# Stick-breaking logs: block 0's three all-ones products become one product over a sum made beforehand

## The reference

```python
z = jnp.einsum('bhtd,bhsd->bhts', q_blk, k_pre) * scale
log_not = jnp.where(valid, jax.nn.log_sigmoid(-z), 0.0)
after = lax.cumsum(log_not, axis=3, reverse=True) - log_not
a = jnp.where(valid, jnp.exp(jax.nn.log_sigmoid(z) + after), 0.0)
outs.append(jnp.einsum('bhts,bhse->bhte', a, v_pre))
```

## Time and profile before

| | |
|---|---|
| median of 3 runs | 1830.77 us (1830.52 to 1831.32) |
| the profiled execution: time | 1831.15 us |
| its span in the profile | 1829.3 us |
| mean granted TensorE clock | 0.997 of full speed |
| instructions | 27260 |

### The profile page before, as it was taken

The page is one execution under the profiler, slowest core; times in us unless marked ns, Lnnn a source line. Parts: engine busy times, 40 slices in busy tenths (PEclk is TensorE's granted clock), DMA queues, the critical chain, the costliest instruction groups (busy, mean ns, idle before and its releaser), DMA issues.

```text
span 1829.3 us, 27260 instructions
## 1 busy us (share of the span) xinstructions
PE 1799.5 (98%) x10778; PEld 1594.2 (87%) x10778; DVE 1281.3 (70%) x1741; ACT 812.4 (44%) x1027; POOL 179.3 (10%) x97
## 2 busy tenths in 40 slices
PE   9999999999999999999999999999999999999996
PEld 8898989887888878788888999998898888999995
DVE  7566665753654737446587878887898786888786
ACT  5666666533223323224453343344545752343342
POOL 2000000010000000000001234230000001224310
PEclk9999999999999999999999999999999999999998
DMA  5012111132222221222512322322476412232331
GB/s 187 26 67 70 46 46 47 47 127 81 70 86 86 83 89 46 92 70 92 183 51 92 116 92 92 115 93 95 113 185 179 144 70 93 97 111 92 103 105 46
DMA packets 25986, 170.25 MB, mean 93 GB/s; under 512 B 2736, under 2 KB 5040, under 8 KB 6320
## 3 DMA queue, kind: packets, MB, share of 16 engines
q1 hardware_dynamic: 24176, 156.51, 24.5%
q0 software_dynamic: 1728, 12.58, 3.3%
HBM read 154.40 MB, written 2.10 MB: 86 GB/s over the span
## 4 chain that ended last, share of the span: by engine, by line
PE 90%; DVE 5%; ACT 2%; issue 2%; DMA 0%; POOL 0%; DVEq 0%; SPq 0%; ACTq 0%
PE psum L705 28%; PE psum L707 28%; PE psum L706 28%; DVE normed L1992 1%; PE psum L907 1%; PE psum L902 1%; PE psum L1049 1%; DVE h L2082 1%; ACT w_hi L1334 1%; PE psum L856 0%; ACT X_hi L1334 0%; PE psum L928 0%; PE psum L1255 0%; DMA h<-in_xfm 0%; ACT std L1334 0%
## 5 line engine op out<-in xcount | busy, mean ns | idle before, releaser
L705 PE MATMUL psum<-X_hi,w_hi 128*128 128x512 f32 (+2 forms) x1392 | 463.7, 333 | 2.8 <-issue 1.2
L707 PE MATMUL psum<-X_hi,w_lo 128*128 128x512 f32 (+2 forms) x1392 | 457.3, 329 | 0.0
L706 PE MATMUL psum<-X_lo,w_hi 128*128 128x512 f32 (+2 forms) x1392 | 457.2, 328 | 0.0
L1975 DVE TENSOR_TENSOR w_lo<-w_raw,w_hi 128x2048 fp32r<-128x2048 f32 x121 | 278.5, 2303 | 93.8 <-ACT w_hi L1334 93.4
L1334 ACT ACTIVATE w_hi<-w_raw 128x2048 fp32r<-128x2048 f32 x133 | 253.6, 1907 | 186.7 <-PE psum L707 149.6
L705 PEld LDWEIGHTS psum<-X_hi,w_hi 128*128 128x128 f32 x1392 | 262.6, 189 | 30.6 <-issue 5.9
L706 PEld LDWEIGHTS psum<-X_lo,w_hi 128*128 128x128 f32 x1392 | 263.0, 189 | 25.9 <-issue 2.4
L707 PEld LDWEIGHTS psum<-X_hi,w_lo 128*128 128x128 f32 x1392 | 262.5, 189 | 23.5
L705 PE MATMUL psum<-M_hi,w_hi 128*128 128x512 f32 x320 | 124.6, 389 | 0.0
L706 PE MATMUL psum<-M_lo,w_hi 128*128 128x512 f32 x320 | 124.6, 389 | 0.0
L707 PE MATMUL psum<-M_hi,w_lo 128*128 128x512 f32 x320 | 124.5, 389 | 0.0
(11 more groups left out here) (364 smaller groups left out, 3989.8 us busy)
## 6 DMA issues: line engine op xcount, KB each, us to landing
w_raw<-in_units SPq DMA_DIRECT2D x140, 1024.0 KB, 4.9
w_lo<-w_raw POOLq DMA_DIRECT2D x12, 1024.0 KB, 6.9
h<-in_xfm SPq DMA_DIRECT2D x4, 528.0 KB, 5.6
h<-in_xfm SPq DMA_DIRECT2D x1, 2112.0 KB, 9.3
decay<-in_dec SPq DMA_DIRECT2D x4, 512.0 KB, 5.6
out<-h SPq DMA_DIRECT2D x4, 264.0 KB, 2.3
out<-h SPq DMA_DIRECT2D x2, 496.0 KB, 2.9
rot<-in_consts SPq DMA_DIRECT2D x1, 528.0 KB, 6.9
```

The source lines that it names most:

```text
L705: nc.tensor.matmul(dst, w2[0], x2[0], start=first, stop=False, skip_group_check=True)
L706: nc.tensor.matmul(dst, w2[0], x2[1], start=False, stop=False, skip_group_check=True)
L707: m = nc.tensor.matmul(dst, w2[1], x2[0], start=False, stop=last, skip_group_check=True)
L1975: v.tensor_tensor(lo, w_raw[at.ring(j)][:, :], as_f32(hi), ALU.subtract).then_inc(w_lo_ready, 1)
```

## The change

Blocks 1 to 3 are now added up ahead of block 0's products: `later2` adds block 3 to the end of block 2, `later1` adds that to the end of block 1, in place in `sp`. The 384 columns that come out are split into `later_hi` (a new copy on ScalarE, into the 48 spare columns of each of the 8 rows of the `X_lo` buffer) and `later_lo` (a new subtraction on VectorE, at the place of `a_f`). Block 0 then has its triangle and one all-ones product with each of the two. The sum for the meta tokens needs one more addition, `all`, in place of three.

```diff
@@ logs, on TensorE
-            for b in (1, 2, 0):
-                pe.wait_ge(hd_dve.sem, hd_dve.at("sp_lo1" if b else "sp_lo0", g))
...
-                for b2 in range(b + 1, BLOCKS):
-                    c0 = P * (b2 - b)
-                    for x in (sp_hi, sp_lo):
-                        m = nc.tensor.matmul(psum[:, 4 + b, c0:c0 + KEY_LEN[b2]], cmat[:, C_ALL, :],
...
+            add_to(2, P, C_ALL, sp_hi, sp_lo, slice(KEY_OFF[3], PACKED)).then_inc(*hd_pe.step("logs1"))
+            pe.wait_ge(hd_dve.sem, hd_dve.at("sp_lo0", g))
+            add_to(0, 0, C_TRI, sp_hi, sp_lo, slice(0, KEY_OFF[1]))
+            pe.wait_ge(hd_dve.sem, hd_dve.at("later_lo", g))
+            nc.tensor.matmul(psum[:, 4, P:SEQ], cmat[:, C_ALL, :], later_hi, start=False, stop=False, skip_group_check=True)
+            nc.tensor.matmul(psum[:, 4, P:SEQ], cmat[:, C_ALL, :], later_lo, start=False, stop=False,
+                             skip_group_check=True).then_inc(*hd_pe.step("logs0"))
@@ softplus, on ScalarE, at its end
+            act.wait_ge(hd_dve.sem, hd_dve.at("later1", g))
+            a(later_hi, sp[:, SEQ:SEQ + LATER].rearrange("p (a b) -> p a b", a=DT), ACT.Copy).then_inc(*hd_act.step("later_hi"))
@@ weights, on ScalarE
-            act.wait_ge(hd_dve.sem, hd_dve.at("all3", g))
+            act.wait_ge(hd_dve.sem, hd_dve.at("all", g))
@@ softplus, on VectorE, behind between()
-            for n, cols in ((1, slice(SEQ, PACKED)), (0, slice(0, SEQ))):
+            def low(n, cols):
                 dve.wait_ge(hd_act.sem, hd_act.at(f"hi{n}", g))
                 v.tensor_tensor(sp_lo[:, cols], sp[:, cols], as_f32(sp_hi[:, cols]), ALU.subtract)\
                     .then_inc(*hd_dve.step(f"sp_lo{n}"))
+
+            def behind(b):
+                own = slice(KEY_OFF[b] + P, KEY_OFF[b + 1])
+                v.tensor_tensor(sp[:, own], sp[:, own], sp[:, KEY_OFF[b + 1]:KEY_OFF[b + 1] + KEY_LEN[b + 1]], ALU.add)\
+                    .then_inc(*hd_dve.step(f"later{b}" if b else "all"))
+            low(1, slice(SEQ, PACKED))
+            dve.wait_ge(hd_dve.sem, hd_dve.at("sp_lo1", g))
+            behind(2)
+            dve.wait_ge(hd_dve.sem, hd_dve.at("later2", g))
+            behind(1)
+            low(0, slice(0, SEQ))
+            dve.wait_ge(hd_act.sem, hd_act.at("later_hi", g))
+            tiles = [x.rearrange("p (a b) -> p a b", a=DT) for x in (later_lo, sp[:, SEQ:SEQ + LATER])]
+            v.tensor_tensor(tiles[0], tiles[1], as_f32(later_hi), ALU.subtract)\
+                .then_inc(*hd_dve.step("later_lo"))
             if then:
                 then()
-
-            for b in range(1, BLOCKS):
-                dve.wait_ge(hd_dve.sem, hd_dve.at(f"all{b - 1}" if b > 1 else "sp_lo0", g))
-                v.tensor_tensor(sp[:, b * P:SEQ], sp[:, b * P:SEQ], sp[:, KEY_OFF[b]:KEY_OFF[b] + KEY_LEN[b]],
-                                ALU.add).then_inc(*hd_dve.step(f"all{b}"))
+            dve.wait_ge(hd_dve.sem, hd_dve.at("sp_lo0", g))
+            behind(0)
```

More of the change, by code:

```diff
@@ L54 @@
 PACKED = sum(KEY_LEN)
+LATER = KEY_LEN[1]
 KEY_BANK = [0, 1, 2, 2]
@@ L259, in build @@
     XM = X_buf[:, :, 0:MROWS]
-    X_lo = sb("X_lo", [P, DT, X_PITCH], F32R, align=256)[:, :, X_PITCH - FULL:]
+    X_lo_buf = sb("X_lo", [P, DT, X_PITCH], F32R, align=256)
+    X_lo = X_lo_buf[:, :, X_PITCH - FULL:]
+    later_hi = X_lo_buf[:, :, 0:LATER // DT]
     acc = sb("acc", [P, DT, SEQ])
@@ L292, in build @@
     sp_all_lo = sb("sp_all_lo", [P, SEQ], F32R, quad)
-    a_f = sb("a_f", [P, PACKED], F32, quad)
+    a_only = ExitStack()
+    a_f = sb("a_f", [P, PACKED], F32, a_only)
+    a_only.close()
+    later_lo = sb("later_lo", [P, PACKED], F32R, quad)[:, 0:LATER]
     a_hi = sb("a_hi", [P, PACKED], F32R, quad)
@@ L438, in build @@
     v_dve = Steps(sem("v_dve"), ["V_lo0", "VM_lo"])
-    hd_act = Steps(sem("hd_act"), ["abs1", "abs2", "abs0", "exp1", "exp0", "ln1", "ln0", "hi1", "hi0", "all_hi",
+    hd_act = Steps(sem("hd_act"), ["abs1", "abs2", "abs0", "exp1", "exp0", "ln1", "ln0", "hi1", "hi0", "later_hi", "all_hi",
                                    "a_part1", "a_part2", "a_hi1", "a_part0", "a_hi0"])
-    hd_dve = Steps(sem("hd_dve"), ["sp1", "sp2", "sp0", "sp_lo1", "sp_lo0", "all1", "all2", "all3", "all_lo", "a_lo1", "a_lo0"])
+    hd_dve = Steps(sem("hd_dve"), ["sp1", "sp2", "sp0", "sp_lo1", "later2", "later1", "sp_lo0", "later_lo", "all", "all_lo",
+                                   "a_lo1", "a_lo0"])
     hd_pe = Steps(sem("hd_pe"), ["scores", "logs1", "logs0"])
@@ L895, in logs, with add_to @@
         def logs(g):
-            for b in (1, 2, 0):
-                pe.wait_ge(hd_dve.sem, hd_dve.at("sp_lo1" if b else "sp_lo0", g))
-                n = KEY_LEN[2] + KEY_LEN[3] if b == 2 else KEY_LEN[b]
-                if b < 3:
-                    for x in (sp_hi, sp_lo):
-                        m = nc.tensor.matmul(psum[:, 4 + b, 0:n], cmat[:, C_TRI, :], x[:, KEY_OFF[b]:KEY_OFF[b] + n],
-                                             start=False, stop=False, skip_group_check=True)
-                for b2 in range(b + 1, BLOCKS):
-                    c0 = P * (b2 - b)
-                    for x in (sp_hi, sp_lo):
-                        m = nc.tensor.matmul(psum[:, 4 + b, c0:c0 + KEY_LEN[b2]], cmat[:, C_ALL, :],
[L908 to L911, removed]
+            def add_to(b, c0, which, hi, lo, cols):
+                for x in (hi, lo):
+                    m = nc.tensor.matmul(psum[:, 4 + b, c0:c0 + cols.stop - cols.start], cmat[:, which, :], x[:, cols],
+                                         start=False, stop=False, skip_group_check=True)
+                return m
+            pe.wait_ge(hd_dve.sem, hd_dve.at("sp_lo1", g))
+            add_to(1, 0, C_TRI, sp_hi, sp_lo, slice(KEY_OFF[1], KEY_OFF[2]))
+            add_to(1, P, C_ALL, sp_hi, sp_lo, slice(KEY_OFF[2], KEY_OFF[3]))
+            add_to(1, 2 * P, C_ALL, sp_hi, sp_lo, slice(KEY_OFF[3], PACKED))
+            add_to(2, 0, C_TRI, sp_hi, sp_lo, slice(KEY_OFF[2], PACKED))
+            add_to(2, P, C_ALL, sp_hi, sp_lo, slice(KEY_OFF[3], PACKED)).then_inc(*hd_pe.step("logs1"))
[5 more added lines that the diff above has]
+                             skip_group_check=True).then_inc(*hd_pe.step("logs0"))
         def meta_scores(t, p):
```

## The result

| | before | after |
|---|---|---|
| median (range), 21 runs each | 1830.95 (1830.39 to 1831.89) | 1834.04 (1832.73 to 1834.73) |
| profiled execution, its span | 1831.15, 1829.3 | 1834.26, 1832.5 |

The ratio is 1.0016, 95% interval 1.0010 to 1.0022: 3.1 us slower. That is within the 0.2% which the forecast called no change, though the interval reaches just past it. The forecast was 1.4 us slower.

The account below looks back on a forecast made before the run. TensorE's matmuls, busy 1799.5 of 1829.3 us, were taken to bound the kernel. Third groups +5.4 and +1.0, first groups -1.4, second and fourth -3.6 sum to +1.4 us: 1832.1 us, range 1827.8 to 1835.3.

Parts of the forecast that it names:

- no change: Whole kernel: a time within 0.2%, 3.7 us, of before; chance 0.77.
- TensorE's saving, 0.45 a group: Block 0's all-ones products: two of 384 columns in place of six save TensorE 0.45 us a group.
- The third groups, +1.80 in three trips and +1.04 in one: ScalarE's copy waits for later1 and delays w_hi, m_f and sp_all_lo: +5.4 us over three trips, +1.0 in the first.
- Where TensorE waits there: Third groups, line 928 in meta_logs: the wait grows to 2.6 us, part perhaps at a quad strip waiting for its bank.
- First groups -0.35, second and fourth -0.45: V_lo behind the late a_lo shrinks the first groups' saving, -1.4 us in all; second and fourth keep theirs, -3.6.
- `later_lo` in time by 0.15 us: Third groups, later trips: later_lo is there at 246.31, its first reader at 246.47; a small miss is absorbed behind.
- The products on 8 runs of 48 columns cost nothing: TensorE's product on such runs: extra price between nothing and 0.18 us in 12 groups, 2.2 us; taken as nothing.
- Rival 2: Copy or subtraction on 8 runs of 48 columns costs more than on a plain tile: 1836; chance 0.12, missed wait included.
- Rival 1 (TensorE's work decides): All 16 groups keep 0.45 us, giving 1823.6 us; chance 0.11.
- Rival 3 (the third groups cost 0.5 to 1 us each): Part of ScalarE's chain behind the copy is faster than added up: 1828 to 1830 us; chance counted within 0.77.

Follow-up runs that it names:

- e1: Kernel before, block 0's six all-ones products cut to two, nothing added on ScalarE or VectorE, contribution of blocks 2 and 3 left out; 1825.59 us.
- e7: Changed kernel, with VectorE making later_hi in place of ScalarE, and sp_all_lo and a_lo made ahead of w_lo in the third groups; 1824.81 us.
- e2: Changed kernel with block 0's six old all-ones products on TensorE; later_hi and later_lo are still made but nothing reads them; 1837.67 us.
- e6: Kernel before, with VectorE's order swapped in the third groups: sp_all_lo and a_lo ahead of w_lo; 1829.59 us.
- e8: Changed kernel, but each trip's third group takes block 0's six old products, without later_hi and later_lo there; 1826.23 us.
- e11: Changed kernel with block 0's six old products in the third groups, and VectorE making the weights' low parts ahead of w_lo; 1824.82 us.
- e9: Changed kernel with 68 warm-up products of 64 columns at the start in place of 36 of 128; 1853.82 us.
- e10: Changed kernel with later_hi on VectorE, the weights' low parts ahead of w_lo, and 68 warm-up products of 64 columns; 1844.32 us.
- e12: Changed kernel, copy still on ScalarE, with VectorE making the weights' low parts ahead of w_lo in the third groups; 1828.57 us.

## Why the forecast held, and where it was short

- **TensorE's saving, 0.45 a group.** Held: -0.45 in every first group, -0.42 to -0.53 in the fourth; by itself (e1) 6.8 us in the sticks.
- **The third groups, +1.80 in three trips and +1.04 in one.** Held: +1.78, +1.77, +1.79 and +1.08. `w_hi` was forecast at 245.64 and came at 245.63, m_f at 249.47 and came at 249.46, `sp_all_lo` at 254.87 and came at 254.84.
- **Where TensorE waits there** was open in the working and wrong among the signs, which had waits of about 2.5 us for `sp_all_lo`. There are two: 1.0 us for `acc` on the way (a strip waits for its bank, since VectorE's pair of sums stands behind the late m_f), and 1.3 at the product. With 0.16 us more than shown for each, that is the 2.6 of the working, and the end is the same, as the second wait ends at a fixed time.
- **First groups -0.35, second and fourth -0.45.** Held in sum: V_lo starts right behind a_lo, and its waits grew from 2.1 to 2.6 us. They stand ahead of the second groups' product, which is why the table has the -0.35 in the second column.
- **`later_lo` in time by 0.15 us** in the third groups of the later trips did not hold: the weight load of the product with `later_hi` waits 0.2 us there, and the product starts 0.03 late. The longer wait behind absorbs it, as the forecast had said.

```profile
PEld psum L919 <- DVE later_lo L2174: 0.6, 3, 0.2
```

- **The products on 8 runs of 48 columns cost nothing.** Shown: the first takes 337 ns like the plain one (338), over all 16 of each, 0.17 to 0.18 us from start to start (0.21 at the three that come late by `later_lo`). Rival 2 falls with it and with the copy at 0.52 and `later_lo` at 0.56 us. The Trainium skill, Advanced Engine Details and Errata, section SBUF Cachelines, is agreed with: full speed on such runs, now on all three engines.

```profile
L919 PE MATMUL psum<-X_lo,cmat x16: 336/337/367, 45.2 to 349.3; 128*128 128x384 f32 x16
L920 PE MATMUL psum<-later_lo,cmat x16: 336/338/343, 45.4 to 349.4; 128*128 128x384 f32 x16
```

- **Rival 1 (TensorE's work decides)** is false for this kernel. For e7, which has the added work and no queue held by it, it nearly holds: less the swap's 1.63, the change brings 6.25 us of the 7.2.
- **Rival 3 (the third groups cost 0.5 to 1 us each)** is false: they cost 1.78. Nothing of ScalarE's chain behind the copy was faster than added up.
- **The step that was short** is the one that was not written: that outside the sticks nothing changes. The sum had +1.4 (1832.17 on the runs' scale, put down as 1832.1), the sticks gave +1.34, and in the profiled execution 1.8 us came from elsewhere: 0.43 from the start-up and 1.33 from the load. So more than half of the 3.1 us stands in no term of the sum, and "no change" was forecast with 0.6 us to spare; that part is luck. Nor is the load chance of one execution: in the eleven kernels with an unchanged start, sticks and load together give the change of the median to 0.5 us (to 0.3 in nine; the changed kernel: 2.67 for 3.09), and the sticks alone miss it by 1.0 to 1.8 us in the seven late ones.

**The late load.** In 14 traces the load was late in all seven in which an instruction packet started 1.2 to 3.7 us behind the start of M_lo, and on time in all seven in which it came 1.9 us or more ahead. Here are the DMA queues of the changed kernel from 1443.8 to 1450.1 us (packets, MB, share); the same view of the kernel before, from 1441.9 to 1447, has no row for q8:

```profile
q1 hardware_dynamic: 228, 1.74, 79.4%
q8 instruction: 1, 0.02, 1.7%
```

The trace keeps more than the view shows. The load is reported done in 16 parts. It is issued 0.15 or 0.16 us behind the start of M_lo in all 14 traces, so no issue is late. In the seven on time, all 16 parts have landed by 5.09 us. In the seven late ones 15 have landed by 5.04, and one alone comes at 6.00 to 6.43, which is when `first_hi` starts. In the five late traces where the instruction packet falls into the full flow of the load, it takes 1.0 us, and meanwhile 15.0 to 15.2 data packets are in flight at a time on average, where it is 16.1 to 16.2 just before. So the packet takes one of 16 places, and one of the 16 parts lands 1.1 to 1.4 us late for it. That the late part is the one behind the packet is inferred, since the trace doesn't say where each went.

That the packet comes when it does because TensorE's stream is 64 products shorter fits e2 and e6 (not shorter, packet at -5.0), e8 and e11 (48 shorter, at -2.0 and -1.9) and the late seven (64 shorter, 1.2 to 3.7). In e9 and e10, with as many as before behind a longer start-up, it is at -9.4 and -9.2. Where within this spread it falls is not explained. The Trainium skill, Runtime: NRT & Kernel Launch, section Instruction fetch mechanics, says that instructions arrive in blocks of 16 KiB by a DMA queue of their own, at a cost that is mostly hidden. By the size of the packets the trace agrees; by the cost, these runs show 1.1 to 1.4 us where a load stands on the path.

**What stays open.** The 0.43 us of the start-up isn't explained; the start-up lasts 26.7 to 27.7 us in the 12 traces where it is unchanged.

## What to carry to other kernels

An operation that is put on a queue costs what is queued behind it, and its own length is the small part: here a copy of 0.52 us brought 1.48 us of waiting ahead of a weight split, and the third groups lost 1.8 each. Before a split goes to the less busy engine, ask on which engine its input is ready when its turn comes: on VectorE, busy 70%, which makes the sum itself, the copy cost less than on ScalarE, busy 45%, which had to wait for it. And where an engine at 98% saves work and the time doesn't move, look for the group that waits for another; leaving that group out (e8) or moving one long, unhurried operation behind the wanted one (e12, and e7 with the copy on VectorE) turned 3 us lost into 3 to 6.5 gained, 1.7 of which the move alone would have brought (e6).

## What the hardware showed that was not expected

- **A start-up of narrow products ran at half pace throughout.** e9, timeline of TensorE from the start:

```profile
1.00 29.27 PE L835 MATMUL psum<-ones 128*128 128x64 f32 x136 [1.00 <-POOL ones L655]
30.07 2.07 PE L827 MATMUL psum<-normed,ones 128*128 128x264 f32 x4
```

  and in the changed kernel:

```profile
1.00 11.19 PE L835 MATMUL psum<-ones 128*128 128x128 f32 x72 [1.00 <-POOL ones L655]
12.19 1.16 PE L827 MATMUL psum<-normed,ones 128*128 128x264 f32 x4
```

  136 instructions of 64 columns took 29.27 us, and 72 of 128 columns 11.19. In the changed kernel the first 28 start 0.21 us apart and the rest, from 7.1 us on, 0.11 apart. In e9 all 136 start 0.21 apart: at the slow pace a product of 64 columns is no shorter than one of 128, and the fast pace doesn't come. The products of 264 columns behind them start 0.44 us apart there, and 0.22 in the changed kernel. That is the ratio of TensorE's two clock levels, 1.2 and 2.4 GHz, with the engine busy in both. The view prints a granted clock of 1.00 for all of these windows, but the trace's clock records begin only at 7.08 us, and at 35.15 in e9, where the pace changes; ahead of its first record the view's 1.00 says nothing. In the 12 traces with the wide products the records begin between 4.1 and 7.2 us.
- **VectorE's copy of 384 fp32 columns took 0.35 us**, its subtraction of the same 0.56 and ScalarE's copy 0.52. I had taken 0.5 for it. The Trainium skill, VectorE: DVE Perf Modes, section Mode 2×_2P — use both read ports for one tensor, has copies from SBUF with one tensor operand at double pace and operations on two tensors not; these rows agree in direction, with 0.56 against 0.35 us, a ratio of 1.6.
